# A SwiGLU feed-forward network whose gate and up projections take seven block products where eight stood

## What is computed

```python
hp = rmsnorm(xp, g_ffn_norm[i]) * (1 + mp[4]) + mp[3]      # context tokens
hs = rmsnorm(xs, g_ffn_norm[i]) * (1 + ms[4]) + ms[3]      # latent tokens
xp = xp + mp[5] * swiglu(hp, w_ffn_gate[i], w_ffn_up[i], w_ffn_down[i])
xs = xs + ms[5] * swiglu(hs, w_ffn_gate[i], w_ffn_up[i], w_ffn_down[i])
# swiglu(h, wg, wu, wd) = (silu(h @ wg) * (h @ wu)) @ wd;  wg, wu: 1024 x 2816, wd: 2816 x 1024, float32
```

## Time and profile before

| | us |
|---|---|
| median of 3 runs | 1720.65 |
| lowest, highest | 1720.02, 1721.17 |
| the profiled execution's own time | 1719.84 |
| its span, first to last instruction | 1718.1 |
| TensorE busy in the span | 1679.1 (98%) |
| weight loads | 1584.2 (92%) |
| VectorE | 878.1 (51%) |
| ScalarE | 676.8 (39%) |
| mean granted TensorE clock | 0.995 |

### The profile page before, as it was taken

How to read it: one execution, slowest core, us unless ns; L and a number is a source line. 1 busy time by engine, 2 the same in 40 slices (tenths; PEclk the granted TensorE clock), 3 DMA queues, 4 the chain that set the end, 5 groups by cost and what they waited for, 6 DMA issues and landing times.

```text
span 1718.1 us, 28029 instructions
## 1 busy us (share of the span) xinstructions
PE 1679.1 (98%) x11500; PEld 1584.2 (92%) x11500; DVE 878.1 (51%) x1429; ACT 676.8 (39%) x1034; POOL 97.4 (6%) x147
## 2 busy tenths in 40 slices
PE   6999999999999999999999999999999999999997
PEld 4878878799999999999989999989999999999997
DVE  5437455664434234444467787786844433344333
ACT  4534535343222112223257777885522221222222
POOL 1111111100000000000010000000000000000000
PEclk9999999999999999999999999999999999999999
DMA  9544444523442232323222222213222222222321
GB/s 312 166 147 145 158 152 132 164 74 116 123 123 83 77 103 77 115 79 92 63 79 79 64 73 64 74 44 106 78 74 73 78 84 67 65 73 73 91 68 61
DMA packets 228438, 170.62 MB, mean 99 GB/s; under 512 B 8723, under 2 KB 209078, under 8 KB 228342
## 3 DMA queue, kind: packets, MB, share of 16 engines
q1 hardware_dynamic: 214262, 120.36, 24.1%
q0 software_dynamic: 14080, 48.90, 8.4%
HBM read 160.32 MB, written 4.72 MB: 96 GB/s over the span
## 4 chain that ended last, share of the span: by engine, by line
PE 94%; DVE 3%; ACT 1%; issue 1%; DMA 1%; SPq 0%; POOL 0%; DVEq 0%; ACTq 0%; POOLq 0%
PE acc L669 79%; PE side L1156 2%; PE side L1201 1%; PE acc L1201 1%; PE side L704 1%; PE work L1130 1%; PE work L704 1%; PE work L1156 1%; PE side L887 1%; DVE x L2261 0%; PE acc L869 0%; PE acc L704 0%; PE acc L921 0%; PE side L869 0%; DVE h_lo L2276 0%
## 5 line engine op out<-in xcount | busy, mean ns | idle before, releaser
L669 PE MATMUL acc<-h_hi,w_hi 128*128 128x320 f32 x2414 | 565.8, 316 | 6.8 <-DVE h_lo L1952 2.0
L669 PE MATMUL acc<-h_lo,w_hi 128*128 128x320 f32 x2414 | 552.1, 310 | 0.0
L669 PE MATMUL acc<-h_hi,w_lo 128*128 128x320 f32 x2414 | 551.8, 310 | 0.0
L669 PEld LDWEIGHTS acc<-h_hi,w_hi 128*128 128x128 f32 x2414 | 402.4, 189 | 37.7 <-issue 26.4
L669 PEld LDWEIGHTS acc<-h_hi,w_lo 128*128 128x128 f32 x2414 | 407.1, 189 | 0.0
L669 PEld LDWEIGHTS acc<-h_lo,w_hi 128*128 128x128 f32 x2414 | 405.9, 188 | 0.0
L1290 ACT ACTIVATE w_hi<-w_raw 128x1024 fp32r<-128x1024 f32 (+4 forms) x186 | 204.4, 1099 | 362.9 <-PE acc L669 354.0
L1886 DVE TENSOR_TENSOR w_lo<-w_raw,w_hi 128x1024 fp32r<-128x1024 f32 (+4 forms) x186 | 238.3, 1281 | 199.1 <-ACT w_hi L1290 196.9
L2321 DVE COPY shift_w<-acc 128x2 f32<-128x2 f32 x88 | 14.0, 159 | 299.8 <-PE acc L669 299.7
L669 PE MATMUL acc<-hid_hi,w_hi 128*128 128x320 f32 x704 | 160.8, 310 | 0.0
L669 PE MATMUL acc<-hid_lo,w_hi 128*128 128x320 f32 x704 | 160.5, 309 | 0.0
(11 more groups left out here) (393 smaller groups left out, 1686.7 us busy)
## 6 DMA issues: line engine op xcount, KB each, us to landing
a_raw<-in_w_ada_dram POOLq DMA_DIRECT2D x80, 512.0 KB, 5.9
w_raw<-in_w_ffn_gate_dram SPq DMA_DIRECT2D x44, 512.0 KB, 3.8
w_raw<-in_w_ffn_up_dram SPq DMA_DIRECT2D x44, 512.0 KB, 3.7
w_raw<-in_w_ffn_down_dram SPq DMA_DIRECT2D x32, 704.0 KB, 4.5
w_raw<-in_w_gla_in_dram SPq DMA_DIRECT2D x24, 512.0 KB, 3.9
w_raw<-in_w_diff_qkv_dram SPq DMA_DIRECT2D x24, 512.0 KB, 3.9
a_left<-in_w_ada_dram SPq DMA_DIRECT2D x8, 512.0 KB, 9.5
a_right<-in_w_ada_dram SPq DMA_DIRECT2D x8, 512.0 KB, 9.9
```

Of the source, the lines that this page charges most:

```text
L669: mm = pe.matmul(out[:, s, 0:HALF + s * more], w[slot][:, k * P:(k + 1) * P], a(k)[:, s * HALF:(s + 1) * HALF + s * more], start=(k == 0 a ...
```

## The change

Weights and inputs of gate and up are seen as one product of 2 x 2 blocks. The 8 input tiles are two groups of JT = 4, the tokens two halves of 320 (each with the two shift columns: HC = 322), and the outputs are gate and up. One level of Strassen's algorithm (Winograd's form) makes the four output blocks of a hidden tile from seven products P1 to P7, each of 4 x 3 = 12 matmuls of 322 columns.

- Weights: for each hidden tile four sums are made by VectorE: two at once (`T13`, 1024 columns), then `T2` and `T4` (512 each). All seven weight blocks of 512 columns are split in high (`weight_hi`) and low (`weight_lo`). SyncE loads the tile as four DMAs (`ff_load`), into two raw buffers used in turn; the buffers of high and low parts are single.
- Inputs: once a layer, three sums are made for each of the 4 tiles and a difference `s3` (`operand_sums`), and five operands of 4 tiles are split (`operand_hi`, `operand_lo`), from `xg`, a scaled copy of `x` (`scaled_x`).
- Outputs: three products are copied out by ScalarE (`kept`); the others add up in PSUM over them, and VectorE adds and scales (`c11`, `c22`, `c21`, `c12_scaled`, `c22_scaled`, `gate_scaled`).
- The FFN runs in four portions of 6, 6, 5 and 5 hidden tiles with a down projection each, of 8 units of 36 or 30 matmuls. In each the first two units run up to their last hidden tile, then both last ones follow (`down_steps`).
- The adaLN blocks stand after hidden tiles 2, 4, 8, 14 and 18 of layer 0. The loops are written out. Several semaphores of the attention are merged into one.

```diff
+JT = 4
+HC = HALF + 2
+PORTIONS = [(0, 6), (6, 12), (12, 17), (17, FT)]
+HT = 6
...
 # SyncE
+            def ff_load(layer, i):
...
+                    sp.wait_ge(ff_low, split_no[layer, i - 2, "P3"] + 1)
+                    sp.wait_ge(ff_low, split_no[layer, i - 2, "P2"] + 1)
+                    sp.wait_ge(ff_added, sum_no[layer, i - 2, "T4"] + 1)
...
+                for w, got, rows in ((w_gate, g_in, (0, 3)), (w_up, u_in, (1, 2))):
+                    src = w[layer].rearrange("(b k p) n -> p b k n", p=P, b=2)
+                    for b, row in enumerate(rows):
+                        sp.dma_start(raw[:, row, :].rearrange("p (k n) -> p k n", k=JT), src[:, b, :, i * P:(i + 1) * P])\
+                            .then_inc(got[s], 16)
...
 # TensorE
+            def product(layer, i, name, a=0, b=JT):
...
+                    if name == "P1" and g > 1:
+                        pe.wait_ge(c12_done, g - 1)
...
+                    elif name == "P5":
+                        pe.wait_ge(u2_kept, g + 1)
...
+                    elif name == "P3":
+                        pe.wait_ge(c22_done, g + 1)
+                for j in range(a, b):
+                    x_high, x_low = ff_operand(name, j)
...
+                    for n, (w, x_part) in enumerate(((high, x_high), (high, x_low), (low, x_high))):
+                        mm = pe.matmul(out, w[:, j * P:(j + 1) * P], x_part,
...
+            def ffn(layer, n, blocks={}):
+                for p, (a, b) in enumerate(PORTIONS):
+                    pe.wait_ge(acc_free[0], FFN[layer] + 4 * p)
+                    product(layer, a, "P1")
+                    product(layer, a, "P7")
+                    if p == 0:
+                        product(layer, 0, "P6", 0, JT - 1)
...
+                        product(layer, 0, "P2", 0, JT - 1)
+                        sum_squares(n)
+                        pe.wait_ge(acc_free[1], FFN[layer])
+                        product(layer, 1, "P1")
+                    for i in range(a, b):
+                        begin = JT - 1 if i == 0 else 0
+                        product(layer, i, "P6", begin)
+                        product(layer, i, "P2", begin)
+                        if 0 < i < b - 1:
...
+                            product(layer, i + 1, "P1")
+                        product(layer, i, "P5")
+                        if i < b - 1:
+                            product(layer, i + 1, "P7")
+                        product(layer, i, "P4")
+                        product(layer, i, "P3")
+                        if i in blocks:
+                            ada_block(blocks[i])
+                    for u in range(2):
+                        down_steps(layer, p, u, 0, b - a - 1)
+                    for u in range(2):
+                        down_steps(layer, p, u, b - a - 1, b - a)
+                    for u in range(2, KD):
+                        turns = layer == 1 and p == len(PORTIONS) - 1
+                        down_steps(layer, p, u, 0, b - a, {2: [lambda: y_turn(u - 2)]} if turns else {})
...
 # ScalarE
+            def ffn_begin(layer, n, m):
+                kept(layer, 0, "P1")
+                weight_hi(layer, 1, "P1")
+                operand_hi(layer, "s2", 3)
+                operand_hi(layer, "h1", 3)
+                operand_hi(layer, "h2", 3)
+                kept(layer, 0, "P7")
+                weight_hi(layer, 0, "P5")
+                weight_hi(layer, 1, "P7")
+                weight_hi(layer, 0, "P4")
+                weight_hi(layer, 0, "P3")
+                act.wait_ge(var_ready, n)
+                act.activation(rstd[:, 0:T], var[:, :], ACT.Ln).then_inc(ln_ready, 1)
...
+            def ffn_period(layer, i, p):
+                a, b = PORTIONS[p]
+                if i > a:
+                    silu(layer, i - 1)
+                    weight_hi(layer, i, "P3")
+                kept(layer, i, "P6")
+                if i + 1 < b:
+                    weight_hi(layer, i + 1, "P6")
...
 # VectorE, layer 1's output projection
-                for k in range(KD - 2):
+                for k in range(4):
                     add_squares(3, k)
...
+                    operands(1, k)
+                for name in ("T13", "T2", "T4"):
+                    weight_sum(1, 0, name)
+                weight_lo(1, 0, "P1")
+                weight_lo(1, 0, "P7")
+                add_squares(3, 4)
+                operands(1, 4)
                 add_to_x(*out_unit(8), KD - 2, 8)
...
+            def ffn_begin(layer, n, m):
+                operand_sums(layer, 7)
+                weight_lo(layer, 1, "P1")
+                operand_lo(layer, "s2", 3)
+                operand_lo(layer, "h1", 3)
+                operand_lo(layer, "h2", 3)
+                add_squares(n, 7)
+                weight_lo(layer, 0, "P5")
+                weight_sum(layer, 1, "T13")
+                weight_lo(layer, 1, "P7")
+                weight_lo(layer, 0, "P4")
+                weight_lo(layer, 0, "P3")
+                weight_sum(layer, 1, "T2")
+                variance(n, var[:, :])
+                newton_step(m, var[:, :], rstd[:, 0:T], sq[0][:, :])
...
+            def ffn_period(layer, i, p):
+                a, b = PORTIONS[p]
+                if i > a:
+                    c12_scaled(layer, i - 1)
+                    weight_lo(layer, i, "P3")
+                    hidden(layer, i - 1)
+                if i + 1 < b:
+                    weight_lo(layer, i + 1, "P6")
+                if i > a:
+                    hidden_lo(layer, i - 1, a)
+                if i + 1 < b:
+                    weight_sum(layer, i + 1, "T4")
+                c11(layer, i)
+                if i + 1 < b:
+                    weight_lo(layer, i + 1, "P2")
+                c22(layer, i)
+                if i + 1 < b:
+                    weight_lo(layer, i + 1, "P5")
+                if i + 2 < b:
+                    weight_lo(layer, i + 2, "P1")
+                    weight_sum(layer, i + 2, "T13")
+                    weight_sum(layer, i + 2, "T2")
+                    weight_lo(layer, i + 2, "P7")
+                c22_scaled(layer, i)
...
+                c21(layer, i)
+                gate_scaled(layer, i)
+                if i + 1 < b:
+                    weight_lo(layer, i + 1, "P4")
...
+                        for u in range(KD):
+                            down_add(layer, p, u)
+                            if u + 2 < KD:
+                                down_lo(layer, p, u + 2)
```

More of the change, by code:

```diff
@@ L551, in _ @@
                 head_load(h + 1, 2)
-            for i in range(3, len(OUT_KT)):
+            for i in range(3, len(OUT_KT) - 1):
                 out_load(i)
@@ L1641, in _ @@
-            projection(GLA_OUT, 1, True)
-            ffn(0, 1, 0, lambda: split_hi(DIF_IN, 0), ADA_FFN, ADA_UP)
+                    for k in range(KD):
+                        if k + 2 < KD:
+                            down_hi(layer, p, k + 2)
+                        elif layer == 0:
+                            split_hi(DIF_IN, k + 2 - KD)
+                        if layer == 0:
+                            scaled_hi(n + 1, k, first)
+                        squares(n + 1, k, lambda: act.wait_ge(acc_free[k % 2], first + k // 2 + 1))
+                        if layer == 1 and k == 0:
+                            act.activation(small[:, 56:57], ones[:, 0:1], ACT.Sqrt)
+                        if layer == 1 and k:
+                            y_copy(k - 1)
@@ new lines, in down_lo, with pairs_lo @@
+            def down_lo(layer, p, u):
+                pair, slot = down_pair(layer, p, u)
+                n = (PORTIONS[p][1] - PORTIONS[p][0]) * P
+                dve.wait_ge(hi_ready, unit(pair, slot) + 1)
+                high, low = down_slot(slot)
+                dve.tensor_tensor(low[:, 0:n], down_raw(p, slot)[:, 0:n], high[:, 0:n].bitcast(F32), ALU.subtract)\
+                    .then_inc(lo_ready, 1)
+            def pairs_lo(layer):
+                for j in range(3):
+                    operand_lo(layer, "h1", j)
+                    operand_lo(layer, "h2", j)
@@ new lines, in projection @@
+                for d in range(2):
+                    dve.wait_ge(st_out[d], 16 * GH)
+                mods_ready(AB * l + 6)
+                add(0)
+                split_lo(first + 1, 0)
+                add(1)
+                operands(0, 0)
+                split_lo(first + 1, 1)
+                split_lo(first + 2, 0)
+                add(2)
+                add_squares(n, 1)
+                operands(0, 1)
+                add(3)
+                add_squares(n, 2)
+                operands(0, 2)
```

882 lines of the change are left out of this document (576 added, 306 removed).

## The result

The changed kernel takes 1704.35 us (median of 4, 1702.81 to 1707.18) beside 1720.91 for the kernel before on the same chip (4 runs, 1720.02 to 1721.25): ratio 0.9906, 95% interval 0.9889 to 0.9924. It is faster by 16.6 us by the medians, half of the forecast 33. The profiled executions differ by 1719.84 - 1704.14 = 15.7 us, so 16.9 us of the forecast's sum are missing.

The account below looks back on a forecast made before the run. TensorE, busy 98% of the span, was taken to bound the kernel. Terms -77.9 + 2 + 14.2 + 21.7 + 10 - 2.6 = -32.6 us from 1719.84 gave 1687.2, forecast 1688 as median; range 1662 to 1722.

Parts of the forecast that it names:

- 44 tiles at 12.43: Steady FFN: 84 matmuls per hidden tile instead of 96, at 148.0 ns each, 1.77 us less a tile, -77.9 us.
- adaLN loads, layer 0: Layer 0's hidden tiles, where adaLN loads share the DMA engines: 2 us of waits in all, bounds 0 and 10.
- start of layer 0: Layer 0's FFN start: TensorE waits 7.2 us at `sum_squares`, 4.9 before P5, 0.8 for c12, clock 1.7: +14.2 us.
- start of layer 1: Layer 1's FFN start: waits at P1, P6 and P2, `sum_squares`, P5 and c12 sum to 20.3, with clock: +21.7 us.
- down projections: Third unit of each down projection waits 1.25 us for the first unit's add and a low part, eight times: +10 us.
- last down projection: Two 1.05 us stands before turns of y go, and one turn less in the tail, -0.5: -2.6 us.
- Does VectorE keep up?: Steady hidden tile: VectorE's list of 11.30 us fits TensorE's 12.43; no steady wait but 2 us in layer 0.
- the 1.9 us: Steady tile: c12 ends 1.6 us into the next period, TensorE needs it at 3.55, so 1.9 us are spare.
- The load: Hidden tile's 1 MB of weights takes 5.6 us from raw buffers free at 2.7, landing at 8.3; T13 takes it at 8.8.
- rival D: Loop of load, sums, splits, load, 12.1 us; if DMAs take longer, TensorE follows at 12.8: +16, 1704 us; chance 0.12.
- Rival C: VectorE sets the period: list 12.56 us, with strict-order waits 13.6 us a tile, time 1739 us; chance 0.15.
- Rival E: Products accumulating in one bank run slower; gain gone at 8.8 ns more per matmul, 1720 us or more; chance 0.04.

Follow-up runs that it names:

- experiment 2: Changed kernel with each down projection's first unit finished after one k step of the second: 1692.70 us, ratio 0.9838 to the kernel before.
- Experiment 4: Changed kernel loading only 64 of 512 columns of adaLN weight blocks 17 to 22, beside layer 0's FFN: 1695.06 us, ratio 0.9857 to the kernel before.
- experiment 1: Changed kernel with three of a hidden tile's four weight DMAs issued about one tile's time earlier: 1691.42 us, ratio 0.9835 to the kernel before.
- 10: Changed kernel with the earlier weight loads, and VectorE's sum T13 made twice in tiles 3 to 21: 1712.70 us, ratio 0.9962 to the kernel before.
- Experiment 6: Changed kernel with ScalarE's copy of the last adaLN block's rows moved earlier in its list: 1701.27 us, ratio 0.9899 to the kernel before.
- second record: The changed kernel itself run again, unedited, as yardstick for three edits: 1705.93 us, ratio 0.9920 to the kernel before.
- experiment 5: Changed kernel with 320 columns, not 322, in 81 of a tile's 84 block products: 1701.41 us, ratio 0.9901 to the kernel before.
- experiment 11: Changed kernel with ScalarE making P3's high part before the silu of the tile before: 1701.53 us, ratio 0.9893 to the kernel before.

## Why the prediction was wrong, point by point

| Step | Predicted, us | Measured, us | Missing |
|---|---|---|---|
| 44 tiles at 12.43 | -77.9 | 12.50: -74.8 | 3.1 |
| adaLN loads, layer 0 | +2 | tiles 4, 10, 20: 4.0 + 4.0 + 1.7 = 9.7 | 7.7 |
| other steady waits | 0 | layer 1, tiles 3, 4, 15: 1.8 | 1.8 |
| start of layer 0 | +14.2 | 16.2, less 0.4 before: 15.8 | 1.6 |
| start of layer 1 | +21.7 | 21.8, less 0.1 before: 21.7 | 0.0 |
| down projections | +10 | 4 x 1.47 + 4 x 1.34, and 0.3 once: 11.5 | 1.5 |
| last down projection | -2.6 | pauses gone -2.1, tail +0.5: -1.6 | 1.0 |

That is 16.7 us. Another 0.5 lies outside the span (2.2 us in this execution, 1.7 before), so the terms overfill the 16.9 by 0.3, which is their error. The tile terms are distances from P6 to P6 over 12.50 (14.44 with an adaLN block); the starts are what the distances of TensorE's matmuls have over 149 ns each, from 372 to 415 and from 1216 to 1266 us; those of the down projections are what experiment 2 took away per portion, layer 0's first one set down as the others.

- **The step that failed is "Does VectorE keep up?", in its price for late loads.** It put +2 us for all waits of the steady part, since "a late load must eat the 1.9 us too". They took 11.5 us, and these 9.5 are more than half of what is missing. Two things were wrong in it, one for each layer.
- **Layer 0, the size of the contention with the adaLN loads.** It was named, its upper bound (10) is what the tiles lost (9.7), its value (2) was a guess without a row. One load of gate weights came 2.5 to 3.4 us late in each stalled tile, more than any room that the walk had. Some 3 of the 9.7 us are the half clock behind two of the pauses, for which the sum had no term. Experiment 4 shows the cause, small adaLN loads and no stall; experiment 1 shows that an earlier load takes it away as well.
- **Layer 1, the 1.9 us "spare".** VectorE's instructions were sized right (distances of 0.60, 0.40, 0.74, 1.32 for 0.61, 0.40, 0.73, 1.27). But the walk had VectorE wait 0.2 us for P3's high part. The rows show 0.60 there, because ScalarE has the silu before it, and the silu waits for VectorE's scaled gate. With that and the waits at `hid_lo` and at P5's low part the two engines' ring is 12.43 us. So the room is a stock that is used once in a portion and is not earned back from tile to tile. It was also smaller: in a tile without waits C12 starts 1.6 us into the next period, where the walk had it end, and P1, due at 3.6, starts 0.63 us after C12 does (457.12 after 456.49), which leaves 1.3 us. The pace of 12.43 is shown by experiments 1 and 10. That short waits add up on it is seen in the changed kernel: in layer 1's tiles 6 to 9 C12 starts 1.59, 1.86, 2.55 and 3.05 us into the next tile, with waits of T13 of 0.18, 0.66 and 0.47 between.
- **The load** was to land at 8.3 for a use at 8.8. A load issued from 1265.89 on was taken by T13 at 1272.38, 6.49 us later and not 5.6: four issues take SyncE 2.0 us, and the up weights land 4.4 us (median) after theirs. That is rival D's loop, and the measured 1704 is D's figure, but by luck: D had every tile at 12.8, where most took 12.50. Outside the adaLN loads it was late by 0.5 us in some tiles, and only the lack of slack made it count.
- **The 3.1 us of the 44 tiles**: the forecast took 148.0 ns a matmul, measured were 148.8. The prediction's other value, 149.1 (12.52 us), lay nearer, and its rows give it: 147.9 ns on average for 320 and 322 by turns, and 9.68 us for 66 matmuls of 320, 146.7 each, leave 149.1 for 322.
- **Rival C**: C's time of 1739 us did not come, but VectorE was nearer to setting the period than I held it: 12.43 for 12.50. The rule of the Trainium skill ("VectorE: DVE Perf Modes", section "The TRN2 errata") would add its latency to each instruction. The trace doesn't agree: independent starts lie 0.60 us apart for 512 columns as in the earlier trace rows. The wait that mattered stood between two engines, and no per-instruction price shows it.
- **Layer 0's start**: VectorE's and ScalarE's times came within 0.4 us (last addition 387.5 for 387.3, the last squares added at 393.3 for 393.1, variance 399.1 for 398.7, U2's copy ended at 402.3 for 402.0). The 7.16 us pause had the predicted size at another place: not `sum_squares` but P6, which waits for ScalarE's copy of P1, queued behind the last square; `sum_squares`, at 394.01, then waited for nothing. The walk had left that copy out. The pause before P5 (4.47 for 4.9) is as predicted, the 0.8 us for C12 did not come. The clock was taken once and came twice: 8.4 us of matmuls at half, 267 to 271 ns apart, lost 3.6 us where 1.7 stood.
- **Layer 1's start**: the size is right by luck. Of its parts only the pause before P5 (4.82 for 4.9) came; P1 and `sum_squares` waited for nothing. The walk missed that the last mixer unit waits 6.09 us for ScalarE's `a_row`, which the change had queued behind the operands' work, and that P6 waits 4.99 for the copy of P1. Experiment 6 shows that the first doesn't matter: VectorE's list reaches that unit's addition only at 1237.07, more than 5 us after TensorE has left the unit, and P6 waits for what follows it.
- **Down projections**: mechanism and size right (pauses of 1.08 to 1.21, or 1.24 to 1.38 from start to start, for 1.25). In the last one the pauses before y's turns are gone, but the tail did not get shorter: from its last matmul to the end of the span 15.10 us where it was 14.62 (14.62 again in the second record).
- **Rival E** fell: 148.8 ns in the steady part, no more than the 149.1 that the rows before give for 322 columns, so what one bank in a row could cost is at most the 0.6 ns that experiment 5 leaves open.
- The range held the time; the median lay 16 us above the forecast, by 9.5 us of waits for loads that I took for covered, 3.1 us of a matmul's price and smaller misses that all went one way.

## What to carry to other kernels

An engine at 90% of a period is not one with 10% to spare: follow the ring it forms with its neighbours, each wait included, and compare that with the period; if they are equal, any late transfer adds up until something resets it. A stall late in a block can be the mark of such a ring, if the lateness grew from tile to tile; one transfer that is later than the room gives the same picture, as in layer 0 here. Issuing the load earlier cured both. When two queues will load at the same time, price it from a row or take the upper bound. At a start bounded by one engine's list, a long pause on another engine may be worth nothing, and moving one item moves the pause.

## What the runs showed of the hardware

- Around the end of each pause of 4 to 7 us TensorE's clock was granted at 0.50 (the 1.2 GHz level) for a stretch; two executions of the changed kernel had 27.3 and 37.5 us of it in the FFN's starts. The same came behind two pauses of 2.19 and 2.23 us, but not behind one of 2.33 us in experiment 2. Among the changed kernel's executions the slowest has the lowest mean clock and the fastest the highest (0.979 at 1707.18 us, 0.985 at 1702.81). A pause thus can cost more than itself, and by differing amounts.
- A matmul with its own weight load at full clock: 148.8 ns for 322 columns in the block products, 147.3 for 320 (experiment 5), and 146.7 for 320 in the down units of both kernels. What the last 0.6 ns come from stays open.
- When 2 MB of adaLN weights on GpSimd's queue start with 1 MB on SyncE's, the 1 MB comes late. In experiment 11 both were issued from 563.5 to 566.5, and T13 could start at 576.4, 11.6 us after the last pair's issue began; a load alone was taken 6.49 us after its first issue. That stretch, with the share of the DMA engines and GB/s at the end:

```profile
566.00:577.00 11.00, 11.00 (x76) 11.00 (x76) 5.46 (x9) 3.40 (x7) 0.36 (x1) 1.00 0.82 277
```
